# Attention scores of two head groups made together, even heads in one PSUM bank and odd heads in the other, causal masks first

## What is computed

```python
# path A (256 tokens are one block, so only the own, causal block counts)
s_own = jnp.einsum('bhtd,bhld->bhtl', qc, k_own) * scale
s_own = jnp.where(own_mask, s_own, -jnp.inf)
p = jax.nn.softmax(scores, axis=-1)
# path B
sc = (jnp.einsum('bhtd,bhsd->bhts', qn, k_nope) + jnp.einsum('bhtd,bsd->bhts', qr, k_rope)) * scale
sc = jnp.where(kpos[None, :] <= qpos[:, None], sc, -jnp.inf)
p = jax.nn.softmax(sc, axis=-1)
# after both
x = x + jnp.einsum('bsd,de->bse', g_a * y_a + g_b * y_b, w_out[l])
x = x + jnp.einsum('bsf,fd->bsd', u * u, w_ff2[l])
```

## Time and profile before

| what | value |
|---|---|
| median of 3 runs | 394.22 us (393.81 to 394.45) |
| profiled execution, span from first to last instruction | 391.2 us |
| PE busy | 379.5 us, 97% of the span |
| DVE busy, ACT busy | 231.1 us, 189.7 us |
| granted clock of PE, mean | 0.996 |
| steps 1 to 12, which hold all scores | about 78.0 to 146.2 us of the span |
| PE L1111 (scores), L1113 (masks) | 64 and 32 matmuls |

### The profile page before, as it was taken

How to read it: one execution, slowest core, us unless ns; L and a number is a source line. 1 busy time by engine, 2 the same in 40 slices (tenths; PEclk the granted TensorE clock), 3 DMA queues, 4 the chain that set the end, 5 groups by cost and what they waited for, 6 DMA issues and landing times.

```text
span 391.2 us, 5693 instructions
## 1 busy us (share of the span) xinstructions
PE 379.5 (97%) x2242; PEld 333.0 (85%) x2242; DVE 231.1 (59%) x293; ACT 189.7 (49%) x315; POOL 17.5 (4%) x39
## 2 busy tenths in 40 slices
PE   5999999999999999999999999999999999999993
PEld 5998889877788888888889898998989899898982
DVE  1976865734656757659477756454564546445325
ACT  4995337934435463336174554453354426444313
POOL 4221000000000010000120000000000000000002
PEclk9999999999999999999999999999999999999998
DMA  7998566724233344506526494656365465620002
GB/s 237 374 383 288 205 210 234 232 92 111 104 109 108 109 137 186 215 0 216 215 93 215 165 363 134 214 184 209 144 214 214 122 215 199 214 107 0 3 0 107
DMA packets 38721, 67.29 MB, mean 172 GB/s; under 512 B 2304, under 2 KB 21504, under 8 KB 38448
## 3 DMA queue, kind: packets, MB, share of 16 engines
q1 hardware_dynamic: 36800, 63.44, 48.1%
q0 software_dynamic: 720, 3.35, 2.5%
q10 hardware_dynamic: 1184, 0.27, 0.3%
HBM read 66.00 MB, written 1.05 MB: 171 GB/s over the span
## 4 chain that ended last, share of the span: by engine, by line
PE 94%; DVE 1%; DMA 1%; ACT 1%; POOL 0%; issue 0%; SPq 0%; ACTq 0%; DVEq 0%; POOLq 0%
PE ps L997 28%; PE ps L999 27%; PE ps L998 27%; PE ps L1004 5%; PE ps L1111 4%; PE ps L1139 3%; DMA xs<-in_x_dram 1%; PE ps L1113 1%; DVE xs L884 1%; ACT xT_hi L396 0%; ACT prob L414 0%; DVE qkT_b L971 0%; ACT qkT_b L396 0%; DVE wlo L675 0%; DVE xT_lo L739 0%
## 5 line engine op out<-in xcount | busy, mean ns | idle before, releaser
L396 ACT ACTIVATE whi<-raw 128x1024 fp32r<-128x1024 f32 (+3 forms) x124 | 120.7, 1009 | 56.6 <-PE ps L999 55.4
L675 DVE TENSOR_TENSOR wlo<-raw,whi 128x1024 fp32r<-128x1024 f32 (+3 forms) x74 | 81.0, 1127 | 22.8 <-ACT whi L396 22.8
L997 PE MATMUL ps<-whi,xT_hi 128*128 128x512 f32 (+3 forms) x208 | 78.8, 379 | 1.9 <-DVE wlo L675 1.6
L919 DVE TENSOR_TENSOR wlo<-raw,whi 128x1024 fp32r<-128x1024 f32 x50 | 60.0, 1222 | 34.0 <-ACT whi L396 34.0
L999 PE MATMUL ps<-whi,xT_lo 128*128 128x512 f32 (+3 forms) x208 | 75.6, 363 | 0.0
L998 PE MATMUL ps<-wlo,xT_hi 128*128 128x512 f32 (+3 forms) x208 | 75.3, 362 | 0.0
L997 PE MATMUL ps<-whi,lat_hi 128*128 128x512 f32 (+1 forms) x180 | 70.0, 389 | 0.0
L998 PE MATMUL ps<-wlo,lat_hi 128*128 128x512 f32 (+1 forms) x180 | 69.5, 386 | 0.0
L999 PE MATMUL ps<-whi,lat_lo 128*128 128x512 f32 (+1 forms) x180 | 69.5, 386 | 0.0
L999 PE MATMUL ps<-xT_hi,wlo 128*128 128x256 f32 x224 | 63.4, 283 | 0.0
L998 PE MATMUL ps<-xT_lo,whi 128*128 128x256 f32 x224 | 63.4, 283 | 0.0
(11 more groups left out here) (96 smaller groups left out, 307.1 us busy)
## 6 DMA issues: line engine op xcount, KB each, us to landing
raw<-in_w_ff_dram SPq DMA_DIRECT2D x32, 1024.0 KB, 5.2
raw<-in_w_in_dram SPq DMA_DIRECT2D x14, 1024.0 KB, 5.9
raw<-in_w_out_dram SPq DMA_DIRECT2D x4, 1024.0 KB, 5.0
gates<-in_b_gate_dram POOLq DMA_DIRECT2D x2, 1024.0 KB, 6.0
raw<-in_w_o_a_dram SPq DMA_DIRECT2D x2, 1024.0 KB, 4.9
raw<-in_w_o_b_dram SPq DMA_DIRECT2D x2, 1024.0 KB, 5.2
raw<-in_w_in_dram SPq DMA_DIRECT2D x2, 576.0 KB, 10.4
raw<-in_w_q_up_dram SPq DMA_DIRECT2D x2, 576.0 KB, 5.6
```

The costliest lines, as they stand in the source:

```text
L396: return nc.scalar.activation(dst, src, ACT.Copy, scale=scale)
L675: nc.vector.tensor_tensor(wlo[:, s, h * w:(h + 1) * w], raw[:, s, h * w:(h + 1) * w], whi[:, s, h * w:(h + 1) * w].bitcast(F32), ALU.subtr ...
L919: nc.vector.tensor_tensor(wlo[:, s, h * w:(h + 1) * w], raw[:, s, h * w:(h + 1) * w], whi[:, s, h * w:(h + 1) * w].bitcast(F32), ALU.subtr ...
L997: nc.tensor.matmul(dst, a_hi, b_hi, start=start, stop=False)
```

## The change

Groups 2p and 2p + 1 become pair p (6 pairs), and `scores(pair)` makes both at once, at the place of the even group: pair 0 in the middle of step 1, the others at the start of steps 3, 5, 7, 9 and 11. Even steps hold no scores. Heads are in their natural order; within a pair, even ones go to bank 4 and odd ones to bank 5, and each group has one half (256 columns) of both banks. First come two mask matmuls, one for each bank, with the triangle repeated (512 columns for tile 0, in two strided pieces of 128 for tile 1); they begin the accumulation, and the score matmuls of all heads are added to it. The pair waits for the exponentials of both groups of the pair before; pair 0 waits for the eleventh copy. `scored` counts pairs: `row_max` of either group waits for its pair, and POOL for the sixth pair. `row_max` reads its half of two banks with one instruction, `exps` reads each head from its bank. All other work keeps its place.

```diff
-HEAD_ORDER = (0, 2, 4, 6, 1, 3, 5, 7)
-GROUPS = [(path, t, HEAD_ORDER[h:h + (4 >> t)]) for path in range(2) for t in range(TT)
+GROUPS = [(path, t, range(h, h + (4 >> t))) for path in range(2) for t in range(TT)
           for h in range(0, 8, 4 >> t)]
+S_BANK = 4
+S_HALF = HALF // 2
...
-            pool.wait_ge(scored, NG)
+            pool.wait_ge(scored, NG // 2)
...
                 for i, h in enumerate(heads):
+                    col = g % 2 * S_HALF + i // 2 * keys
                     e = nc.scalar.activation(prob[:, g % 2, i * keys:(i + 1) * keys],
-                                             ps[:, 4 + g % 2, i * keys:(i + 1) * keys], ACT.Exp,
+                                             ps[:, S_BANK + i % 2, col:col + keys], ACT.Exp,
...
-                dve.wait_ge(scored, g + 1)
-                nc.vector.tensor_reduce(negmax[:, g, 0:len(heads)],
-                                        ps[:, 4 + g % 2, :].rearrange("p (h k) -> p h k", h=len(heads)),
+                dve.wait_ge(scored, g // 2 + 1)
+                cols = slice(g % 2 * S_HALF, (g % 2 + 1) * S_HALF)
+                nc.vector.tensor_reduce(negmax[:, g, 0:len(heads)].rearrange("p (j b) -> p b j", b=2),
+                                        ps[:, S_BANK:S_BANK + 2, cols]
+                                        .rearrange("p b (j k) -> p b j k", j=len(heads) // 2),
                                         AX_X, ALU.max, negate=True).then_inc(max_ready, 1)
...
-            def scores(g):
-                path, t, heads = GROUPS[g]
-                keys, bank = P * (t + 1), 4 + g % 2
-                if g < 2:
-                    pe.wait_ge(qkT_ready, (10, 11)[g])
+            def scores(pair):
+                path, t, _ = GROUPS[2 * pair]
+                keys = P * (t + 1)
+                heads = [h for g in (2 * pair, 2 * pair + 1) for h in GROUPS[g][2]]
+                if pair == 0:
+                    pe.wait_ge(qkT_ready, 11)
                 else:
-                    pe.wait_ge(p_ready, g - 1)
-                if g == NG // 2:
+                    pe.wait_ge(p_ready, 2 * pair)
+                if pair == NG // 4:
                     pe.wait_ge(qkT_ready, 12)
+                n = HALF // keys
+                for b in range(2):
+                    dst = ps[:, S_BANK + b, :].rearrange("p (j k) -> p j k", j=n)[:, :, t * P:keys]
+                    nc.tensor.matmul(dst, ident_h[:, :], bcast(causal[:, :], n), start=True, stop=False,
+                                     skip_group_check=True)
                 for i, h in enumerate(heads):
-                    dst = ps[:, bank, i * keys:(i + 1) * keys]
+                    dst = ps[:, S_BANK + i % 2, i // 2 * keys:(i // 2 + 1) * keys]
...
-                    nc.tensor.matmul(dst, q[:, t * P:(t + 1) * P], k[:, 0:keys], start=True, stop=False)
-
-                    m = nc.tensor.matmul(dst[:, t * P:keys], ident_h[:, :], causal[:, :], start=False, stop=True)
+                    m = nc.tensor.matmul(dst, q[:, t * P:(t + 1) * P], k[:, 0:keys], start=False, stop=True,
+                                         skip_group_check=True)
                 m.then_inc(scored, 1)
...
-                if 0 < s - G_SLOT < NG:
-                    scores(s - G_SLOT)
+                if 0 < s - G_SLOT < NG and (s - G_SLOT) % 2 == 0:
+                    scores((s - G_SLOT) // 2)
                 proj(c, k)
```

## The result

The changed kernel takes 387.97 us in the median (387.82 to 388.31) beside 394.17 for the kernel before: a ratio of 0.9851 (95% interval 0.9839 to 0.9863), 6.2 us faster. Run once more among the experiments, on a chip where the kernel before takes 393.64 us, it took 387.87 (0.9852, 0.9837 to 0.9866), 5.8 us faster. Forecast were 389.8 us, a gain of 4.4, and a range that ended at 388.6. The direction was right; the gain was too small.

The account below looks back on a forecast made before the run. PE, busy 97% of the span, was taken as the bound. Savings of 2.13 + 2.92 + 0.35 + 0.22 = 5.62 us less 1.2 of waits gave 4.4: 394.2 - 4.4 = 389.8 us, range 388.6 to 391.7.

Parts of the forecast that it names:

- waits: PE ahead of `values(0)` in step 2: about 1.1 us idle until group 0's probabilities are copied, 1.2 in all.
- streams come at the pace of the loads, 0.107 each: Pairs 1 and 2, odd head streaming beside even one: four heads take 1.07 us, the pair 1.70, saving 1.46 each.
- bring nothing if loads go one after the other: Pair 0: loads as long as streams, so two row halves gain nothing; 16 streams take 1.71 us, the pair 2.57.
- The price of entering and leaving the 64-partition form: Path A's score blocks: emptying 0.09 us and a bare load 0.11 on entering, the same again before the projection.
- The full overlap: Rival, path A: loads of both row halves overlap too, pair 0 saves 0.75 us more, 389.0 us; chance 0.12.
- the change between bf16 and float32: Path B's pairs 3, 4 and 5: 0.07 us for one change of format beside the masks' streaming.
- The tie in step 10: The probabilities' copy of step 10, behind gate rows and an `o_norm`, is nearest to being late: 0 to 0.3 us.
- the turnaround rival: Rival: PE waits for the shared banks before every pair; at 1.2 us, six cost 7.2, 395.8 us; chance 0.025.
- in line: Rival, path A's tile 1 pairs: the row halves never stream side by side; saves 3.1, 391.1 us; chance 0.25.
- emptying at each change of half: Rival: each change of row half empties PE, heads cost 0.41 and 0.63 us as before; 393.7 us; chance 0.07.
- The clock: Rival: after the wait one step runs at 1.2 instead of 2.4 GHz, costing 5.7 us, 395.5 us; chance 0.015.
- The time around the span: Outside the profiled span: the runs' median stands 3.0 us above the span, taken as untouched by the change.

## Why the prediction was right or wrong

The terms, in us of PE. "After" counts from the start of the masks to the first projection matmul behind the scores, and what that matmul takes beyond its usual distance to the next (0.33 against 0.23 behind path A; 0.43 against 0.31 in pairs 4 and 5):

| term | before | after, predicted | after, measured | saved, predicted | saved, measured |
|---|---|---|---|---|---|
| pair 0 | 4.70 | 2.57 | 1.63 + 0.10 = 1.73 | 2.13 | 2.97 |
| pairs 1 and 2, each | 3.16 | 1.70 | 1.39 + 0.10 = 1.49 | 1.46 | 1.67 |
| pair 3 | 2.64 | 2.29 | 2.13 | 0.35 | 0.51 |
| pairs 4 and 5, each | 2.12 | 2.01 | 1.76 + 0.12 = 1.88 | 0.11 | 0.24 |
| sum | | | | 5.62 | 7.30 |
| waits | | | | -1.2 | -1.12 - 0.22 |
| net | | | | 4.4 | 6.0 |

The stretch from step 1 to step 12 gave 5.83, so the table closes to 0.15.

- **The bound, right.** PE's work set the time, all that PE saved less its waits came out at the end, and nothing was given back behind step 12.
- **The step that failed: "streams come at the pace of the loads, 0.107 each", and "bring nothing if loads go one after the other" for pair 0.** They don't go one after the other: loads for the two row halves start together, and a pair takes what one group takes on one half. That is 0.84 in pair 0 and 0.42 in pairs 1 and 2 together. The price of entering and leaving the 64-partition form, 0.40 a time in the sum, held. I had taken the distance of loads in the earlier trace rows as the bound of a load path, but each of those pairs of loads was for one and the same row half; the rows could not speak of two. The full overlap stood among the rivals with 0.12 and 0.75 us, right in its mechanism and for pair 0 in its size; it left out the 0.42 of pairs 1 and 2. The Trainium skill's rule (TensorE: Matmul & The Clock Gate, Part 3: Packing small matmuls), that a pack on different row groups takes hardly longer than one of its matmuls, is what the traces here show for float32, with 1.09 us for 16 streams on two halves and 1.09 for 8 on one.
- **Path B, mis-sized.** I took 0.07 for the change between bf16 and float32 and 0.23 for a block of 512 columns. Pair 4's two masks take 0.22 together (119.89 to 120.11), no more than their streaming, and pair 3's 0.43. Over the three pairs that is 0.26 us; the streams, summed at 0.11 each in pair 3, were 0.16 shorter. Together 0.4 us.
- **The wait, right.** Its place (`values(0)`), its releaser (the copy of the probabilities, DVE L797) and its size: 1.12 us from the end of the projection's stream (87.27) to 88.39, against 1.1. Its cause is shown, since the order that takes the copy out from behind the half unit takes 1.1 us off. The tie in step 10 was a gap of 0.22, within the 0 to 0.3 given. No other pair waited, so the turnaround rival fell; so did in line (the mask in between costs 3.5) and emptying at each change of half.
- **The clock, right for this kernel.** It stayed up over the wait.
- **The time around the span, a small error.** I took 3.0 us from the difference of the span of before to the median of other executions. Execution by execution, for both kernels, it is 2.2. The median of before in the first comparison, 394.2, lies 0.5 above the one beside the experiments; so the forecast missed by 1.8 us there, and the sum itself by 1.4 to 1.6.

With the measured terms in it the sum is 7.3 - 1.3, or 6.0 us: 388.2. The range should have reached the rival that it had named, 389.0, with that rival's own unknowns below it.

## What to carry to other kernels

Where heads of 64 lie on both row halves, let neighbours in PE's list be on different halves (here they also wrote different banks; one bank for both was not tried), and keep full-height matmuls out from between them: two halves then cost what one does, loads included. Before taking work off PE in a stage, look at what chain of other engines ran under it; here 1.1 of 7.3 us came back as a wait, and putting one copy, and the maximum before it, ahead of one half unit of weights on DVE won it back. When a chain of two engines is reordered, walk it through both lists: moving the exponentials too made it longer.

## What the runs showed of the hardware that I had not expected

- PE brings a matmul of the other row half forward past several of its list: with four even streams of 256 columns ahead of the odd ones, all eight still took 1.07 us. With eight even streams of 128 columns ahead, the sixteen took 1.64 in place of 1.09.
- Entering and leaving the 64-partition form costs 0.3 us in the block (1.41 for a mask of 0.23 and streams of 0.86; 1.26 for 0.11 and 0.85) and 0.1 at the first projection matmul behind it: 0.4 a time, about as much as one head's score product with 128 keys took in before. The sum had this price; new is that part of it falls into the first matmul behind the block.
- A stall of 4.7 us went with 6.8 us at half the clock; kernels with waits of 1.0 and 2.2 us had a lower mean clock in some executions (0.986 with the mask between, 0.987 at the least with exponentials ahead), the changed one with its wait of 1.0 in none of eight. Without its wait the kernel with the mask between stayed at 390.3 us in four executions. That the waits bring the lower clock is likely, not shown.
